# Attention stage: order of the score, rotary and pooling products on TensorE, and of the weights that feed them

## The reference, cut to what matters

```python
cq, ckv_raw, kpe, u = split(h @ w_in)                  # 384, 256, 64, 512 columns
q = (rmsnorm(cq) @ w_uq).reshape(b, s, 4, 128 + 64)    # per head: 128 plain, 64 rotary columns
k_nope, v = expand_kv(rmsnorm(ckv), w_ukv)             # per head 128 + 128
s = einsum('bqhd,bkhd->bhqk', q_nope, k_nope) + einsum('bqhr,bkr->bhqk', q_pe, k_pe)
o = softmax(s * scale) @ v
pooled = einsum('bsgc,gcd->bsgd', multiscale_pool(u), w_pool) * pool_scale   # 4 groups of 128
x = x + g1 * (concat([o, pooled]) @ w_out)             # 1024 x 1024
```

## Time and profile before

| | |
|---|---|
| three runs | 1378.53, 1379.96, 1382.36 us |
| profiled execution, span | 1380.1 us |
| TensorE busy | 1349.4 us (98%), 12464 matmuls |
| VectorE, ScalarE, GpSimd busy | 369.6, 248.7, 28.3 us |
| mean granted TensorE clock | 0.991 |
| DMA, mean | 338 GB/s |

### The profile page before, as it was taken

The page is one execution under the profiler, slowest core; times in us unless marked ns, Lnnn a source line. Parts: engine busy times, 40 slices in busy tenths (PEclk is TensorE's granted clock), DMA queues, the critical chain, the costliest instruction groups (busy, mean ns, idle before and its releaser), DMA issues.

```text
span 1380.1 us, 27730 instructions
## 1 busy us (share of the span) xinstructions
PE 1349.4 (98%) x12464; PEld 688.0 (50%) x12464; DVE 369.6 (27%) x599; ACT 248.7 (18%) x397; POOL 28.3 (2%) x60
## 2 busy tenths in 40 slices
PE   6999999999999999999999999999999999999997
PEld 4758799997958633333333333433333333333332
DVE  4435655554434410021121112112102111111212
ACT  3334644443332400000000000010000000000001
POOL 0210000000120000000000000000000000000000
PEclk9999999999999999999999999999999999999999
DMA  9979986554573999999999999999999999999980
GB/s 352 347 282 338 354 292 206 184 195 135 228 277 127 408 351 417 392 363 375 421 403 387 420 409 363 421 351 359 403 421 385 389 420 387 385 420 414 344 363 32
DMA packets 112249, 466.51 MB, mean 338 GB/s; under 512 B 9946, under 2 KB 48644, under 8 KB 76292
## 3 DMA queue, kind: packets, MB, share of 16 engines
q1 hardware_dynamic: 111152, 463.80, 86.2%
q10 hardware_dynamic: 980, 0.94, 0.2%
HBM read 463.33 MB, written 1.38 MB: 337 GB/s over the span
## 4 chain that ended last, share of the span: by engine, by line
PE 95%; DVE 3%; DMA 1%; ACT 1%; issue 1%; SPq 0%; DVEq 0%; ACTq 0%
PE ps L2037 42%; PE ps L2052 21%; PE ps L1653 5%; PE ps L1654 5%; PE ps L1655 5%; PE ps L1687 2%; PE ps L1599 2%; PE ps L1855 1%; PE ps L1856 1%; PE ps L1854 1%; PE ps L1985 1%; PE ps L1969 1%; PE ps L1778 1%; PE ps L1622 1%; PE ps L1678 1%; PE ps L1680 1%
## 5 line engine op out<-in xcount | busy, mean ns | idle before, releaser
L2037 PE MATMUL ps<-ering,xg 128*32 128x512 f32 (+1 forms) x6144 | 582.1, 539 | 0.0
L2037 PEld LDWEIGHTS ps<-ering,xg 128*32 128x32 f32 x6144 | 197.9, 110 | 374.7 <-issue 374.6
L2052 PE MATMUL ps<-ering,eT 128*32 128x512 f32 x2688 | 290.7, 592 | 0.0
L2052 PEld LDWEIGHTS ps<-ering,eT 128*32 128x32 f32 x2688 | 86.9, 110 | 197.8 <-issue 197.8
L1653 PE MATMUL ps<-hx,high 128*128 128x256 f32 x560 | 155.9, 278 | 2.6 <-DVE hx L1092 2.6
L1655 PE MATMUL ps<-hx,low 128*128 128x256 f32 x560 | 155.3, 277 | 0.0
L1654 PE MATMUL ps<-hx,high 128*128 128x256 f32 x560 | 155.3, 277 | 0.0
L1038 DVE TENSOR_TENSOR low<-ring,high 128x1024 fp32r<-128x1024 f32 (+1 forms) x104 | 122.5, 1202 | 73.1 <-ACT high L742 73.0
L976 ACT ACTIVATE sg<-ps 128x512 f32<-128x512 f32 (+1 forms) x48 | 26.1, 544 | 522.6 <-PE ps L2037 522.6
L742 ACT ACTIVATE high<-ring 128x1024 fp32r<-128x1024 f32 (+1 forms) x104 | 105.0, 1039 | 64.7 <-PE ps L1655 31.1
L1461 DVE TENSOR_TENSOR sq<-sg,ps 128x512 f32<-128x512 f32 (+1 forms) x48 | 29.8, 621 | 302.5 <-PE ps L2037 300.5
(11 more groups left out here) (250 smaller groups left out, 858.8 us busy)
## 6 DMA issues: line engine op xcount, KB each, us to landing
ering<-in_moe_w_down SPq DMA_DIRECT2D x112, 1024.0 KB, 10.8
ering<-in_moe_w_gate SPq DMA_DIRECT2D x64, 1024.0 KB, 8.3
ering<-in_moe_w_up SPq DMA_DIRECT2D x64, 1024.0 KB, 10.3
ering<-in_moe_w_gate SPq DMA_DIRECT2D x64, 768.0 KB, 6.0
ering<-in_moe_w_up SPq DMA_DIRECT2D x64, 768.0 KB, 7.8
ring<-in_w_ada SPq DMA_DIRECT2D x40, 1024.0 KB, 9.1
ring<-in_ffn_w_gate SPq DMA_DIRECT2D x11, 1024.0 KB, 7.8
ring<-in_ffn_w_up SPq DMA_DIRECT2D x11, 1024.0 KB, 10.1
```

What stands on the lines that cost most here:

```text
L2037: last = mm(ps[32 * c:32 * c + 32, bank, 0:width].rearrange("p (n r) -> p n r", r=64), xg[:, kk, at, 32 * g:32 * g + 32], w[t][:, c, :, :] ...
L2052: last = mm(ps[32 * group:32 * group + 32, bank, :], eT[s][:, g, 2 * i + odd, :], w[:, odd, 512 * half:512 * (half + 1)], start=(s, i) == ...
```

## The change

- The rotary query columns of two heads are computed in turn: for each step of the contraction first the even head, then the odd one.
- Scores by kind: for two heads the four products over 128 channels, then the four rotary products, heads in turn.
- The product of the pooled channels with `w_pool` moves ahead of the keys, into banks 0 and 1, and its high and low parts (ScalarE, VectorE) move with it; the keys of head 3, which use bank 1, wait for the low part (`pooledl_ready`). `w_pool` moves ahead of `w_ukv` in the stream.
- The pooled halves of output blocks 0 and 1 are computed after the scores, ahead of `turn_p`; those of blocks 2 and 3 ahead of block 0's part for the heads. The output blocks use banks 7, 1, 0, 3.
- Both `turn_p` calls follow each other, with p of head 1 turned into bank 4 and p of head 3 into bank 3.
- Splitting ahead of the softmax is cut to two pieces in layer 0 (the other two come after the turned p) and to four in layer 1 on ScalarE (before: seven asked for); on VectorE, layer 1, two of the four are done between the copies of v.
- `ol_ready` is raised for each pair of heads, and block 0 waits for them one by one; the wait for `kv_out_ready` at block 4 goes.

```diff
-POOL_BANK = (7, 3)
+POOL_BANK = (0, 1)
+OUT_BANK = (7, 1, 0, 3)
+TURNED_P = (0, 4, 2, 3)
+SPLIT_AHEAD = (2, 4)
...
-        out += latents[:-2] + [("uq", l, 0), ("uq", l, 1)] + latents[-2:] + [("ukv", l, 0)]
-        out += ada("softmax", l) + [("pool", l, 0)]
+        out += latents[:-2] + [("uq", l, 0), ("uq", l, 1)] + latents[-2:] + [("pool", l, 0), ("ukv", l, 0)]
+        out += ada("softmax", l)
...
+                act.wait_ge(direct_used, 4 * l + DIRECT_USED["pool", 0])
+                for g in range(NG):
+                    last = A(hx[:, NH + g, 0, :], ps[:, POOL_BANK[g // 2], ...
+                last.then_inc(pooledh_ready, 1)
                 act.wait_ge(kv_done, 3 * l + 1)
...
-                upto(min(PIECE0[ITEM["ukv", l, 0]] + PIECES, within("ukv", l, 0)))
+                upto(min(PIECE0[ITEM["ukv", l, 0]] + SPLIT_AHEAD[l], within("ukv", l, 0)))
...
+                A(pT[:, 0, :], ps[:, TURNED_P[0], 0:3 * 128], ACT.Copy)
+                A(pT[:, 1, :], ps[:, TURNED_P[1], 0:3 * 128], ACT.Copy).then_inc(pT_low_ready, 1)
+                upto(PIECE0[ITEM["ukv", l, 0]] + 4)
...
+                dve.wait_ge(pooledh_ready, l + 1)
...
                     last = V.tensor_copy(v[:, i, :], ps[:, b, :])
+                    if l and i < 2:
+                        upto(PIECE0[ITEM["ukv", l, 0]] + i + 1)
                 last.then_inc(v_ready, 1)
-                upto(min(PIECE0[ITEM["ukv", l, 0]] + 4, within("ukv", l, 0)))
+                upto(min(PIECE0[ITEM["ukv", l, 0]] + SPLIT_AHEAD[l], within("ukv", l, 0)))
...
+            def project_out(l, m, pooled):
+                hi, lo = piece(first("out", l, m // 2) + m % 2, KD)
+                out = half_bank(OUT_BANK[m // 2], m % 2)
+                for k in range(NH, KD) if pooled else range(NH):
+                    if m == 0 and not pooled and k % 2 == 0:
+                        pe.wait_ge(ol_ready, 2 * l + k // 2 + 1)
+                    xh, xl = hx[:, k, 0, :], hx[:, k, 1, :]
+                    mm(out, hi[:, k, :], xh, start=m % 2 == 0 and k == NH, stop=False, skip_group_check=True)
+                    mm(out, hi[:, k, :], xl, start=False, stop=False, skip_group_check=True)
+                    last = mm(out, lo[:, k, :], xh, start=False, stop=k == NH - 1, skip_group_check=True)
+                if not pooled:
+                    last.then_inc(pieces_used, 1)
...
-                for h in range(NH):
-                    a, pp = h * (NOPE + ROPE) + NOPE, slice(64 * (h % 2), 64 * (h % 2) + 64)
-                    last = direct(ps[pp, 3, h // 2 * N2:(h // 2 + 1) * N2], [w[:, a:a + ROPE] for w in wq], cqT)
+                for j in range(NH // 2):
+                    for k, wk in enumerate(wq):
+                        for h in (2 * j, 2 * j + 1):
+                            a, pp = h * (NOPE + ROPE) + NOPE, slice(64 * (h % 2), 64 * (h % 2) + 64)
+                            last = mm(ps[pp, 3, j * N2:(j + 1) * N2], wk[:, a:a + ROPE], cqT[:, k, :], start=k == 0, stop=k == KQ - 1)
...
+                pe.wait_ge(pool_ready, l + 1)
+                wp = slot(arrived("pool", l, 0), NG, 128)
+                for g in range(NG):
+                    last = mm(half_bank(POOL_BANK[g // 2], g % 2), wp[:, g, :], poolT[:, g, :], start=True, stop=True)
+                last.then_inc(direct_used, 1)
                 w = slot(arrived("ukv", l, 0), KK, NH * (NOPE + VD))
                 for h, b in enumerate((4, 5, 3, 1)):
+                    if h == NH - 1:
+                        pe.wait_ge(pooledl_ready, l + 1)
...
-                for h in range(NH):
-                    pp = slice(64 * (h % 2), 64 * (h % 2) + 64)
-                    for b, (a, z) in enumerate(((0, T), (T, 3 * T))):
-                        mm(ps[:, SCORES_BANK[h], a:z], qT[:, h, b * T:(b + 1) * T], kT[:, h, a:z], start=True, stop=False)
-                        last = mm(ps[:, SCORES_BANK[h], a:z], q2[pp, h // 2, b * T:(b + 1) * T], kpeT[pp, a:z], start=False, stop=True)
-                    if h % 2:
-                        last.then_inc(s_done, 1)
+                keys = ((0, T), (T, 3 * T))
+                for i in range(2):
+                    for h in (2 * i, 2 * i + 1):
+                        for b, (a, z) in enumerate(keys):
+                            mm(ps[:, SCORES_BANK[h], a:z], qT[:, h, b * T:(b + 1) * T], kT[:, h, a:z], start=b == 0, ...)
+                    for b, (a, z) in enumerate(keys):
+                        for h in (2 * i, 2 * i + 1):
+                            pp = slice(64 * (h % 2), 64 * (h % 2) + 64)
+                            last = mm(ps[:, SCORES_BANK[h], a:z], q2[pp, i, b * T:(b + 1) * T], kpeT[pp, a:z], start=False, stop=True, ...)
+                    last.then_inc(s_done, 1)
                 mod_rows(beside[1:])
+                for m in range(2):
+                    project_out(l, m, True)
...
-                turn_p((0, 1), (0, 1))
-                pe.wait_ge(p_ready, 2 * l + 2)
-                pe.wait_ge(pool_ready, l + 1)
-                wp = slot(arrived("pool", l, 0), NG, 128)
...
+                for i in range(2):
+                    pe.wait_ge(pn_ready, 2 * l + i + 1)
+                    turn_p((2 * i, 2 * i + 1))
...
-                pe.wait_ge(pooledl_ready, l + 1)
+                for m in range(2, 4):
+                    project_out(l, m, True)
                 for m in range(KD):
                     if m == 4:
                         mod_rows(items_at("out", l))
-                        pe.wait_ge(kv_out_ready, l + 1)
-                    project(half_bank(m // 2, m % 2), first("out", l, m // 2) + m % 2, OUT_ORDER)
+                    if m >= 4:
+                        project_out(l, m, True)
+                    project_out(l, m, False)
```

More of the change, by code:

```diff
@@ L1257, in mixer @@
                 dve.wait_ge(pT_done, 2 * l + 2)
[L1258 to L1265, removed]
+                V.tensor_copy(pT[:, 2, :], ps[:, TURNED_P[2], 0:3 * 128])
+                V.tensor_copy(pT[:, 3, :], ps[:, TURNED_P[3], 0:3 * 128]).then_inc(pT_high_ready, 1)
+                upto(PIECE0[ITEM["ukv", l, 0]] + 4)
                 for i in range(2):
                     dve.wait_ge(oh_ready, 2 * l + i + 1)
-                    last = V.tensor_tensor(hx[:, 2 * i:2 * i + 2, 1, :], ps[:, HEADS_BANK[i], :].rearrange("p (h t) -> p h t", h=2), hx[:, 2 * i:2 * i + 2, 0, :], ALU.subtract)
-                last.then_inc(ol_ready, 1)
+                    V.tensor_tensor(hx[:, 2 * i:2 * i + 2, 1, :], ps[:, HEADS_BANK[i], :].rearrange("p (h t) -> p h t", h=2), hx[:, 2 * i:2 * i + 2, 0, :], ALU.subtract).then_inc(ol_ready, 1)
                 for j in range(4):
@@ L1647, in project @@
                         pe.wait_ge(hx_ready, waits + k // 4)
[L1648 to L1651, removed]
                     xh, xl = hx[:, k, 0, :], hx[:, k, 1, :]
@@ new lines, in mixer @@
+                for i in range(2):
+                    for h in (2 * i, 2 * i + 1):
+                        for b, (a, z) in enumerate(keys):
+                            mm(ps[:, SCORES_BANK[h], a:z], qT[:, h, b * T:(b + 1) * T], kT[:, h, a:z], start=b == 0, stop=False, skip_group_check=True)
+                    for b, (a, z) in enumerate(keys):
+                        for h in (2 * i, 2 * i + 1):
+                            pp = slice(64 * (h % 2), 64 * (h % 2) + 64)
+                            last = mm(ps[:, SCORES_BANK[h], a:z], q2[pp, i, b * T:(b + 1) * T], kpeT[pp, a:z], start=False, stop=True, skip_group_check=True)
+                    last.then_inc(s_done, 1)
@@ L1793, in mixer, with turn_p @@
                 mod_rows(beside[1:])
-                def turn_p(heads, banks):
-                    for h, b in zip(heads, banks):
+                for m in range(2):
+                    project_out(l, m, True)
+                def turn_p(heads):
+                    for h in heads:
                         for i in range(3):
-                            last = nc.tensor.transpose(ps[:, b, i * 128:(i + 1) * 128], p[:, h, i * 128:(i + 1) * 128], ident)
+                            last = nc.tensor.transpose(ps[:, TURNED_P[h], i * 128:(i + 1) * 128], p[:, h, i * 128:(i + 1) * 128], ident)
@@ L1799, in turn_p @@
                     last.then_inc(pT_done, 1)
-                pe.wait_ge(pn_ready, 2 * l + 1)
-                turn_p((0, 1), (0, 1))
-                pe.wait_ge(p_ready, 2 * l + 2)
-                pe.wait_ge(pool_ready, l + 1)
-                wp = slot(arrived("pool", l, 0), NG, 128)
-                for g in range(NG):
-                    last = mm(half_bank(POOL_BANK[g // 2], g % 2), wp[:, g, :], poolT[:, g, :], start=True, stop=True)
-                last.then_inc(direct_used, 1)
-                pe.wait_ge(pn_ready, 2 * l + 2)
@@ L1812, in mixer @@
-                turn_p((2, 3), (2, 4))
+                for i in range(2):
+                    pe.wait_ge(pn_ready, 2 * l + i + 1)
+                    turn_p((2 * i, 2 * i + 1))
                 for h in range(NH):
```

16 lines of the change are left out of this document (7 added, 9 removed).

## The result

The changed kernel took 1371.23 us in the median of its first four runs (1366.73 to 1373.35) against 1381.16 of the kernel before (four runs, 1378.53 to 1384.93), a ratio of 0.9931 with a 95% interval of 0.9912 to 0.9950. Five more runs beside nine of the kernel before gave 1369.22 against 1379.34, 0.9921 (0.9908 to 0.9935). So it is 10 us, 0.7 to 0.8%, faster. The forecast was 10.4 us and 1369.7. One execution of experiment 8 took 2003.87 us at a granted clock of 0.652, where every other one stands at 0.988 or above; it is in none of the figures here.

The account below looks back on a forecast made before the run. TensorE, busy 1349.4 of 1380.1 us, was taken as the bound. Rotary columns 1.0, scores 6.7, waits 0.6 and 0.6 and clock 1.45 summed to 10.4 us, giving 1369.7; range 1366 to 1375.5.

Parts of the forecast that it names:

- Rotary query columns in turn: Rotary query columns, 3.22 us a layer: alternating heads gains 0.5 us a layer, 1.0 in both.
- Scores by kind: Score products: from 8.35 to 5.0 us a layer, gain 3.35 (2.4 to 3.65), 6.7 us in both layers.
- Rival A: Only changes of shape are saved, row halves do not overlap: 6.0 us gained, 1374.1 us; chance 20%.
- 0.2 us for a change of shape: Scores: each change between 128 and 64 rows costs 0.20 us; of 16 a layer, four (0.8 us) remain.
- Pooling product ahead of the keys: Pooling product moved before the keys: cost 0, as three heads of keys cover its low part with 0.4 us to spare.
- rival C: Head 3's keys wait for the pooled low part and the gain is eaten: about 1378 us; chance 7%.
- Splitting and v in layer 1: VectorE's splitting between copies of v makes the layer 1 scores wait: cost 0.35 us (0 to 0.6).
- Filling the softmax: Pooled halves (2.8 us) fill TensorE's softmax waits: 1.02 us (layer 0) and 1.47 (layer 1) go, 0.1 left at most.
- What is late next: With both `turn_p` together, TensorE waits 0.4 us in each layer for ScalarE's copies, at the value products.
- The clock in layer 1: Without the 1.47 us gap the clock's fall in the softmax does not come: 1.45 us gained (0 to 1.45).
- B: Full overlap of the halves and one more fall of the clock gone: 13 us gained, 1367 us; chance 12%.
- D: Slower: `w_out` 0 lands late and turned p, values and output queue behind it, say 1384 us; chance 3%.

Follow-up runs that it names:

- experiment 8: On top of experiment 7, the pooled half of output block 1 stands between the two `turn_p`: 1367.89 us against 1379.89, ratio 0.9914.
- experiment 4: Changed kernel with the rotary query columns head by head, six instructions in a row on one column half: 1368.66 us in one run.
- experiment 10: Changed kernel with odd heads' rotary query columns also written to partitions 0 to 63, so on one column half: 1375.45 us in one run.
- experiment 9: Changed kernel with the rotary scores of all heads on partitions 0 to 63, one half of the rows: 1370.68 us in one run.
- experiment 1: Kernel before the change with the scores by kind and nothing else: 1380.49 us against 1381.28, ratio 1.0003.
- experiment 7: Changed kernel with the last two score groups exchanged, so two changes of row shape between groups instead of three: 1366.34 us in one run.
- experiment 6: Changed kernel with the weight stream in the old order, `w_pool` behind the softmax items: 1381.99 us in one run.
- experiment 11: On top of experiment 8, three pieces instead of four split ahead of the softmax of layer 1: 1367.42 us against 1379.34, ratio 0.9915.
- experiment 5: Changed kernel with the pooled halves of output blocks 0 and 1 behind the values instead of amid the softmax: 1370.91 us in one run.
- experiment 2: Changed kernel with the rotary scores of a pair head by head instead of in turn: 1370.73 us in one run.
- experiment 3: Changed kernel with the scores in the old order, kind after kind for each head and block: 1375.64 us in one run.
- experiment 12: The changed kernel again without an edit, run beside experiment 11: 1369.22 us.

## Why the prediction was right

- **Rotary query columns in turn**: 0.5 us a layer forecast, 0.48 measured, and shown to be column halves side by side (experiments 4 and 10). The forecast did not say why the old order took 0.134 us an instruction and not 0.216; its halves overlapped already, but for two instructions at either end.
- **Scores by kind**: 5.0 us forecast, 4.73 measured (gain 3.62, forecast 3.35). The step was under-sized in the rotary part, 0.8 us for a pair where 0.65 is right: the row halves overlap wholly. For halves side by side the Trainium skill ("TensorEngine Tiling (Array Packing)", Theoretical Speedup) gives up to twice the speed, and experiment 9 agrees, with 0.65 us against 1.3. The Trainium skill ("TensorE: Matmul & The Clock Gate", LDWEIGHTS) gives a weight load a price by its columns, and the forecast asked what would follow if the loads of the two halves came one after the other: 0.86 us a pair without the shape changes. These runs show less: the eight loads of a rotary group take 0.52 us together (406.30 us in experiment 1), the group 0.65. Rival A (no overlap) falls.
- **0.2 us for a change of shape**: shown by experiment 7, and in experiment 9 it stays when the overlap is gone.
- **Pooling product ahead of the keys**: no wait was forecast and none came; rival C falls. What the forecast treated in two sentences, the order of the weights, proved to have the highest price: 11 us if `w_pool` stays where it was (experiment 6).
- **Splitting and v in layer 1**: 0.35 us forecast, 0.2 measured; experiment 11 removes it.
- **Filling the softmax**: both waits went, as forecast. The forecast gave it 0.6 + 0.6 us as waits removed. Experiment 5 prices it from the other side, at 0.36 and 2.2 us: in layer 1 the shorter scores alone make the wait longer (3.8 us in experiment 1), so part of their 3.6 us belongs to the filling and the splitting. Experiment 1 is the plainest form of this: none of the 7.2 us of shorter scores reaches the end without the two; how they share it was not measured. The terms of a sum like the forecast's hold only together.
- **What is late next**: 0.4 us ahead of the values forecast, 0.31 measured, in both layers; experiment 8 removes it.
- **The clock in layer 1**: no fall in the softmax, as forecast, and the 1.45 us are in what was measured. That the wait of 1.47 us was what brought the fall is not shown. The clock fell behind waits of 4.45 and 3.8 us in experiment 1 and of 7.9 us in experiment 6, but not behind a wait of 1.47 us in experiment 5. Here the forecast was right in the effect, and the cause it gave is open.
- **Sum**: 4.5 us forecast for layer 0, 4.5 and 4.6 measured in two profiles. There the terms measured one by one (0.48 + 3.62 + 1.02 - 0.31) make 4.8, so some 0.2 to 0.3 us was lost at a place that was not looked for. For layer 1 5.9 were forecast and 6.5 measured like for like; the terms (0.48 + 3.62 + 1.47 - 0.31 - 0.2 + 1.45) make 6.5, and the 0.6 over the forecast are the terms above that were taken small. Both stretches gained 11.1, the medians 9.9 and 10.1 us, the forecast said 10.4. The two intervals of the ratio reach from 6.9 to 12.7 us, so the medians agree with both. That the forecast stands so near the medians is in part luck: the terms inside the stretches add up to more, and the rest of the span moves by more than the difference.
- **Rivals B and D**: B's full overlap came, its further fall of the clock less did not show in the medians. D (slower through a late transfer) did not occur: `w_out` 0 was issued at 83.6 us and landed 13.0 us later, at 96.6, and its first half block began at some 105.3. Its mechanism is real, though, at another place: in experiment 6 it is `w_pool`.

## What to carry to other kernels

Group products by the shape of their tile (each change costs 0.2 us here) and let short products for different rows or columns stand near each other in the program: the halves then run beside each other. Here it was enough that the other half's next instruction stood no more than four behind. When TensorE gets shorter ahead of a softmax, look in the same step at what VectorE and ScalarE still have in their queues and at what TensorE can do meanwhile: here the gain was zero without the two together. A part that moves ahead needs its weights ahead as well: one line of the stream cost 11 us. Judge such edits by the stretch in the trace, not by the total, if the total carries a few microseconds of luck from stages that are not touched.

## What the runs showed that was not expected

- Four instructions in a row on one half of the rows lose nothing (experiment 2), six in a row on one half of the columns take 0.48 us more than the 2.74 in turn (experiment 4). The count alone would explain both, as experiment 4 says; six in a row on rows, or four on columns, were not run.
- The output blocks of layer 1 take one of two lengths with the same instructions and the clock at 1.00. From the transposes of the latents to the norm, the changed kernel in its first and its second profile:

```profile
418.75:440.06 21.31, 21.31 (x186) 1.00 0.30 107
```

```profile
414.65:436.69 22.04, 22.04 (x186) 1.00 0.29 103
```

  21.31 and 22.04 us for the same 186 matmuls. In the long form a product of 256 columns starts every 0.118 us, in the short one every 0.113. The long form was seen in the kernel before and in experiments 1, 2, 3, 6, 8 and 12, the short one in the first profile of the changed kernel and in 4, 5, 7, 9, 10 and 11. Layer 0 has both in every execution, blocks 0 to 3 mostly at one pace and blocks 4 to 7 at the other. It goes with the execution, not with the kernel; its cause was not looked for.
- The stretch before the query columns of layer 0 varied from 69.1 to 73.5 us among profiles though no kernel changed its products, in part with the granted clock in it (0.71 from 65 to 70 us in the profile after, 1.00 in the one before).
